# The gate unit between the third branch's units, and key pages ahead of that branch's weights

## The reference

```python
h = rmsnorm(x, norm_mix_pre)
z = h @ w_in          # queries | K/V of 3 branches | branch gates | S5 channels | merge gates
q, kv, gn, u, gm = split(z)             # kv: compressed, selected, window branch; gn: 16 heads x 3
pos = einsum('sd,sdh->h', pe, w1)       # position sums of the compression, for keys and values
pre = first[:, :-1] + second[:, 1:] + pos
kc = gelu(pre) @ w2                     # compressed keys (and values), from paged raw rows
s = q . k of all paged keys             # the sample sequences' scores on the selected branch
g = sigmoid(gn)
o_nsa = g[0] * o_cmp + g[1] * o_slc + g[2] * o_win
```

## Time and profile before

| | us |
|---|---|
| median of three runs | 1245.1 |
| profiled execution | 1256.66 |
| its span, first to last instruction | 1254.9 |
| TensorE matmul busy | 1212.6 |
| VectorE busy | 826.2 |
| GpSimd busy | 338.7 |
| ScalarE busy | 307.6 |

### The profile page before, as it was taken

One profiled execution on the slowest core, in us unless ns is written; L12 is line 12 of the kernel. 1 busy time (PEld: TensorE's weight loads), 2 busy tenths in 40 slices (PEclk: granted clock), 3 DMA queues, 4 the chain that ended last, 5 costly groups with the idle time before them and its releaser, 6 DMA issues.

```text
span 1254.9 us, 19475 instructions
## 1 busy us (share of the span) xinstructions
PE 1212.6 (97%) x7266; PEld 990.7 (79%) x7266; DVE 826.2 (66%) x1376; ACT 307.6 (25%) x729; POOL 338.7 (27%) x404
## 2 busy tenths in 40 slices
PE   6999989999999899999999999999999999999997
PEld 5889757778887566666788888878888888888886
DVE  6999432348988788887764665686755554566555
ACT  6484201120011666665211111040000000000002
POOL 4952343322220132322011211001211113423540
PEclk9999989999999899999999999999999999999999
DMA  9343564577667335336642232511211311221101
GB/s 246 96 139 103 184 147 146 160 283 273 243 250 254 93 115 178 110 118 200 250 140 63 67 118 81 205 67 59 93 67 67 134 68 67 92 110 67 68 1 68
DMA packets 122093, 166.03 MB, mean 132 GB/s; under 512 B 36448, under 2 KB 90528, under 8 KB 117648
## 3 DMA queue, kind: packets, MB, share of 16 engines
q1 hardware_dynamic: 103408, 104.72, 26.3%
q0 software_dynamic: 8080, 50.58, 11.1%
q10 hardware_dynamic: 10512, 9.49, 2.3%
HBM read 159.29 MB, written 13.84 MB: 138 GB/s over the span
## 4 chain that ended last, share of the span: by engine, by line
PE 90%; DVE 4%; ACT 2%; issue 2%; DMA 1%; SPq 0%; ACTq 0%; DVEq 0%
PE PS L2644 48%; PE PS L2179 14%; PE PS L2374 9%; PE PS L2156 5%; PE PS L2522 3%; PE PS L2491 3%; PE PS L2325 2%; PE PS L2555 1%; DMA stream<-in_w_in 1%; DVE small L1846 1%; PE PS L2353 1%; PE PS L2201 1%; PE PS L2309 1%; PE PS L2527 1%; DVE QO L1915 0%
## 5 line engine op out<-in xcount | busy, mean ns | idle before, releaser
L2179 PE MATMUL PS<-hT,stream 128*128 128x260 f32 (+1 forms) x768 | 175.4, 387 | 4.0 <-issue 1.6
L2644 PE MATMUL PS<-R,stream 128*128 128x260 f32 x752 | 173.5, 382 | 0.0
L2179 PEld LDWEIGHTS PS<-hT,stream 128*128 128x128 f32 (+1 forms) x768 | 143.5, 189 | 36.5 <-issue 9.7
L2644 PEld LDWEIGHTS PS<-R,stream 128*128 128x128 f32 x752 | 142.8, 190 | 21.9
L2644 PE MATMUL PS<-R 128*128 128x260 f32 x592 | 135.6, 383 | 0.0
L2644 PEld LDWEIGHTS PS<-R 128*128 128x128 f32 x592 | 112.1, 190 | 17.5 <-DVE R L1898 0.4
L2374 PE MATMUL PS<-R 128*128 128x256 f32 (+1 forms) x544 | 118.8, 379 | 1.4 <-ACT small L1113 1.0
L2644 PE MATMUL PS<-R,QO 128*128 128x260 f32 x496 | 113.8, 383 | 1.4 <-DVE QO L1898 1.4
L2374 PEld LDWEIGHTS PS<-R 128*128 128x128 f32 x544 | 101.4, 194 | 15.8 <-issue 1.7
L1986 DVE TENSOR_TENSOR R<-PS,R 128x260 f32<-128x260 f32 x100 | 42.5, 426 | 100.6 <-PE PS L2644 99.4
L2644 PEld LDWEIGHTS PS<-R,QO 128*128 128x128 f32 x496 | 93.8, 190 | 16.8 <-DVE QO L1898 2.2
(11 more groups left out here) (454 smaller groups left out, 1865.2 us busy)
## 6 DMA issues: line engine op xcount, KB each, us to landing
stream<-in_cache_kv_slc SPq DMA_DIRECT2D x128, 128.0 KB, 2.1
stream<-in_w_mlp_up SPq DMA_DIRECT2D x8, 2048.0 KB, 8.3
stream<-in_w_mlp_down SPq DMA_DIRECT2D x8, 2048.0 KB, 8.7
stream<-in_w_in SPq DMA_DIRECT2D x4, 2048.0 KB, 9.6
stream<-in_state_kv_win SPq DMA_DIRECT2D x16, 512.0 KB, 5.9
stream<-in_w_in SPq DMA_DIRECT2D x8, 1024.0 KB, 18.6
out_kv_win_sample<-in_state_kv_win POOLq DMA_DIRECT2D x1, 8176.0 KB, 43.0
R<-in_cache_kv_slc SPq DMA_DIRECT2D x56, 128.0 KB
```

What stands on the lines that cost most here:

```text
L2179: ins = M(pair(u)[0:w, hf, 0:HALF], lhs[k], rhs[k][:, HALF * hf:HALF * hf + HALF], start=(k == 0), stop=(k == n - 1))
L2644: ins = M(product_of(w, i)[:, c0:c1], lhs[:, k, :], rhs[:, k, c0:c1], start=(k == 0), stop=(k == nk - 1))
```

## The change

Three things are moved, none is added or taken out.

```diff
-    plan += [("win", (C_KV + KVW * c, 512), 1, 0) for c in range(3)]
+    plan += [("win", (C_KV + KVW * c, 512), 1, 0) for c in range(2)]
     plan += [("win", (C_GN, 3 * NH), 1, 0)]
+    plan += [("win", (C_KV + KVW * 2, 512), 1, 0)]
     plan += [("cmp", (NB, 0), 4, 0)]
...
             prev = (c, m)
+            if prev == (2, 0):
+                rest.append(("gemm", ("win", (C_GN, 3 * NH)), 0, 3 * NH, ("gn",)))
+            if prev == (2, 1):
+                rest += [("trg",), ("pos",)]
     rest.append(("tr", *prev))
-    rest.append(("gemm", ("win", (C_GN, 3 * NH)), 0, 3 * NH, ("gn",)))
-    rest += [("pos",), ("trg",)]
...
                     if arg[0] == C_KV + 2 * KVW:
+                        key_loads(7, 8, 9, 10, 11, 12, 13)
+                    if arg[0] == C_GN:
                         key_loads(4, 5, 6)
                         compression_weights()
-                        key_loads(7, 8, 9)
-                    if arg[0] == C_GN:
-                        key_loads(10, 11, 12, 13)
```

## The result

The changed kernel is slower by a third of a percent: 1249.66 us in the median of 17 runs (1243.16 to 1253.26) against 1244.29 us for the kernel before (17 runs, 1242.36 to 1248.2). The medians lie 5.4 us apart; the ratio used from here on is taken over all runs and is 1.0033, 4.1 us, with a 95% interval of 1.0023 to 1.0044. The forecast was no change, 1244 us. The effect is under 0.5%, but its interval leaves 1 out, and the forecast had no mechanism for a loss of this kind: it had put the term that made it at nothing.

A forecast was written before the change was run, and what follows sets the result against it. PE, busy 97% of the span, was taken as the bound. From the median of 1245.1 us, +0.3 (wait before layer 1) and -1.5 (clock), all else nothing, gave 1244 us; range 1238 to 1251.

The forecast's parts named there:

- the cover of key tile 7: Fourth key scores: tile 7's pages, behind the 2 MB, land 4 to 8 us later, still before the scores; cost nothing, thinnest cover.
- the 9.2 us disturbance: Third key scores from 169.13 and what follows: 6.6 + 2.0 + 0.6 us lost in the profiled execution, perhaps absent from timed runs.
- The prediction's own signs of being wrong: PE waiting for stream buffer or key tiles near 196, third scores beyond 178 or whole with the median moving, clock 0.5 beside sums.
- The clock at layer 1: Start of layer 1: the fall to 1.2 GHz over 266.6 to 270.5 goes, -1.5 us.
- the end of the stage: End of projections: key scores come last, PE waits 1.35 us for VectorE's first permutation against 1.04 before, +0.3 us.
- The slower one: Stall at the third key scores (169) lasts through the 2 MB burst to 183.2: +7.7 us, 1251.7 us; 10%.
- The faster one: Stall at the third key scores goes as keys 4 to 6 arrive earlier: -9.2 us, 1234.8 us; 8%.
- The fixed gap: About 6.2 us between a profile's total and reported time; by it 5.4 us of the 11.6 would be left for stalls.
- The clock rival: Clock falls at layer 1 all the same, or behind the sums in the middle, unit (2, 2) paying 1.5 us: 1245.5 us; 25%.
- weak work: Middle of projections: 0.71 us of transposes, 2.35 scores, about 0.5 gate transposes, 1.98 one-column sums in a row, perhaps lowering the clock.
- the DMA share at 134 to 142: Sign of being right: DMA share low there, the 2 MB burst having moved to about 175.
- The 2 MB are hidden: Third branch's weights land by some 183 to 190 and are wanted at 216.63: 26 us to spare, no cost.

The follow-up runs named there:

- the loads alone: Kernel before with only SyncE's order changed: pages of keys 4 to 6 and compression weights ahead of the third branch's 2 MB; ratio 1.0028 to the kernel before.
- tile 7 first: Changed kernel with SyncE issuing the four pages of key tile 7 ahead of the third branch's 2 MB; ratio 0.9997 to the kernel before.
- the two shown: Traces of the changed kernel with key tiles 7 to 9 ahead of the 2 MB (ratio 0.9999) and of the changed kernel unchanged, run again (1.0024).
- tile 8 ahead: Changed kernel with the pages of key tile 8 issued ahead of those of tile 7, both behind the 2 MB; ratio 1.0062 to the kernel before.

## Why the prediction was wrong

**The step that failed** is the cover of key tile 7: "their transposition ends by 187 to 192, and the key scores that read them start at 196.35. Nothing". The landing was right. The tile was forecast 4 to 8 us later than 181.06 and came at 186.18, 5.1 later (6.7 later within the stage, 53.9 against 47.2); it was transposed by 188.5. The due time was wrong. 196.35 was read from the one execution with the 9.2 us disturbance ahead of those scores. In the kernel before, run again, they start at 187.25, 53.0 us into the stage. In the changed kernel's trace that is 132.28 + 53.0 = 185.3, and 188.5 is 3.2 us too late. The text argued a few paragraphs further down that the disturbance may be absent from the timed runs, took its 9.2 us as a rival's gain, and did not take it out of the due time. Taken out there, 196.35 - 9.2 = 187.2 against 187 to 192: a wait of 0 to 5 us, which is the result. The prediction's own signs of being wrong did name a wait for the key tiles there. And the warning was in the numbers from the start: 1256.66 us lies 8 us above 1248.2, the slowest of the three runs known then and of all 17.

**The clock at layer 1** (-1.5 us) was mis-sized from the same execution. The kernel before, run again, has 10.75 us there, as its variant with the loads alone has; the fall showed in one of the three traces with the old order of units, so there was mostly nothing to win back. What the end of the stage does by itself is the other term: forecast 1.35 us of waiting in place of 1.04; measured 1.43 in place of 0.50, so +0.9 us and not +0.3 or, with the clock, -1.2. Without a wait at the fourth scores the stage, counted up to layer 1, takes 123.4 us with tile 7 first (256.18 - 132.74) and 122.3 before (256.48 - 134.22). So by these two traces the moved units bring no gain, but a loss of some 1 us that the timings can't tell from nothing.

**The rivals.** The slower one named another mechanism, a stall of instruction supply that would last through the burst. It didn't happen: the third scores take 2.60 us, and PE is busy 8.85 of the 9.00 us of the burst. The faster one had nothing to win: the stall is in one of twelve traces. The fixed gap weighed under the slower rival does not enter the 11.6 us, as 1256.66 and 1245.1 are both reported times; span and reported time lie 1.8 us apart here (1254.9 and 1256.66, 1248.8 and 1250.64). The clock rival was partly true. Behind the sums in the middle it fell in three of nine traces of the changed order of units: the two shown, and that with tile 8 ahead. It costs the unit behind them 1.4 us (8.70 - 7.28, with tile 8 ahead), 1.7 (8.97 - 7.28) and 3.0 (10.32 - 7.28) then. No wait of PE stood there in any of the nine, so what the prediction held against this rival did not protect from it. The 5.5 us that it calls weak work hold some 1.2 of transposes beside scores and sums, and no run here takes the parts apart.

**The rest held**, but for one sign: the DMA share at 134 to 142 was to be low and is 0.80. The 2 MB are hidden, with no wait at 210.39. The permutations follow as worked out: 2.37, 0.27, then the third without a wait for its gather. Gate unit, sigmoids and sums bring no wait where they stand now.

In time, 3.1 us of wait, 1.6 of clock and 0.9 at layer 1 make 5.6 us for the trace of the changed kernel. Its stage, counted up to layer 1, is 5.9 us longer than in the kernel before, run again (128.1 against 122.3). The medians lie 5.4 apart, the ratio gives 4.1 (0.0033 x 1244). How the wait and the clock differed among the timed runs is not known: the wait was 2.45 and 3.14 in two traces, and half-clock stretches in later stages come and go between traces. Why the first trace of the kernel before had its disturbance stays open too.

## What to carry to other kernels

A due time read from a trace is as good as what ran ahead of it. Where a trace holds a disturbance, and above all where its execution lies well above the median, take the disturbance out of every later time before you call a transfer hidden. Margins of a queue are worked out from a stage's own start, as landing against due time for the first item behind what is moved in, not for the item that is moved. When a 2 MB load can stand on either side of a few small ones, put the ones due first ahead: here it took moving one tile's loads and gave the loss back.

## What the runs showed of the hardware

A wait of PE of 2.5 to 4.5 us at the fourth key scores was followed by the 1.2 GHz level in all four traces that had one (changed twice, loads alone, tile 8 ahead). Beyond the wait itself that cost 1.6 us in both traces of the changed kernel, 2.6 with tile 8 ahead and 2.8 with the loads alone. The wait of 1.43 to 1.54 us ahead of layer 1 brought no fall in nine traces. In the old order the wait there, right behind the position sums and gate transposes, was 1.04 us once, with a fall, and 0.50 us twice, without one. Behind the sums in the middle, with no wait at all, the clock fell in three of nine traces of the same rows. So one trace gives neither the chance of such a fall nor its price.

Two MB in front of key pages on SyncE's queue delayed them by 4.8 to 6.7 us (53.2 to 53.9 in the stage, against 47.2 to 48.4 without), one MB by 1.1 to 2.3 (49.5), less than half of it. GpSimd's gathers, which do not stand in that queue, were held up less: those issued from 172 to 177.5 landed in 3.2 to 6.7 us beside the burst (both traces of the changed kernel), and in 2.8 to 3.1 us in the kernel before, run again, where the burst was over by then.
